# Two-block transformer kernel, one core: order of the first transfers, of the bias-row products and of the unread products at the head

## What is computed

```python
def rmsnorm(x, g):
    y = xf * lax.rsqrt(jnp.mean(xf * xf, axis=-1, keepdims=True) + EPS)
    return y * g
# layer 0 of the first block
h = h + even_mixer(rmsnorm(h, even_norm1[0]), even_w_in[0], ...)
qa, ka, va, qd, kd, vd = split_cols(h @ w_in, EVEN_IN_SPLIT)
bias = jnp.take(bias_table, rel_bucket(dist), axis=0)
```

## Times and profile before

| what | value |
|---|---|
| median of 3 runs | 3155.56 us (3153.17 to 3160.29) |
| profiled execution | 3161.49 us |
| its span, first to last instruction | 3159.6 us |
| PE busy | 96% of the span |
| DVE, ACT, POOL busy | 44%, 25%, 53% |
| mean granted TensorE clock | 0.983 |

### The profile page before, as it was taken

One profiled execution on the slowest core, in us unless ns is written; L12 is line 12 of the kernel. 1 busy time (PEld: TensorE's weight loads), 2 busy tenths in 40 slices (PEclk: granted clock), 3 DMA queues, 4 the chain that ended last, 5 costly groups with the idle time before them and its releaser, 6 DMA issues.

```text
span 3159.6 us, 44388 instructions
## 1 busy us (share of the span) xinstructions
PE 3033.1 (96%) x14692; PEld 2387.0 (76%) x14692; DVE 1399.9 (44%) x2391; ACT 792.1 (25%) x1451; POOL 1660.6 (53%) x1254
## 2 busy tenths in 40 slices
PE   8998999999899999989999999999889999999998
PEld 6767888886578888756678878888657688878886
DVE  3254444223444442452533476640744334576622
ACT  3342221113332210144421122210253411132201
POOL 4334666663156667423346656666323266646674
PEclk9998999999999999999999999999999999999999
DMA  6262223322022233211312222333112222223232
GB/s 161 77 173 67 93 94 106 110 90 74 21 73 93 97 102 110 70 34 53 102 61 99 83 75 95 99 104 103 48 41 75 67 90 100 83 73 100 94 115 77
DMA packets 99603, 274.90 MB, mean 87 GB/s; under 512 B 38126, under 2 KB 38894, under 8 KB 99490
## 3 DMA queue, kind: packets, MB, share of 16 engines
q1 hardware_dynamic: 97328, 269.07, 26.6%
q10 hardware_dynamic: 2162, 4.36, 0.8%
HBM read 269.66 MB, written 11.54 MB: 89 GB/s over the span
## 4 chain that ended last, share of the span: by engine, by line
PE 70%; DVE 3%; ACT 2%; issue 2%; DVEq 0%; ACTq 0%
PE PA L470 11%; PE PA L472 10%; PE PA L471 10%; PE PB L470 9%; PE PB L472 8%; PE PB L471 8%; PE O L736 2%; PE S L693 2%; PE T L604 2%; PE O L502 1%; DVE tmps L1398 0%; DVE hl L1359 0%; PE PB L753 0%; ACT probs L1128 0%; DVE strip L1782 0%
## 5 line engine op out<-in xcount | busy, mean ns | idle before, releaser
L452 POOL TENSOR_TENSOR wl<-raw,wh 128x1024 fp32r<-128x1024 f32 (+2 forms) x416 | 1128.0, 2711 | 33.4
L449 POOL TENSOR_TENSOR zero<-zero 128x1 f32<-128x1 f32 x416 | 82.7, 199 | 1434.3 <-PE PA L472 703.2
L470 PE MATMUL PA<-hh,wh 128*128 128x512 f32 x1392 | 567.1, 407 | 26.4 <-DVE hl L1359 7.1
L472 PE MATMUL PA<-hh,wl 128*128 128x512 f32 x1392 | 550.0, 395 | 0.0
L471 PE MATMUL PA<-hl,wh 128*128 128x512 f32 x1392 | 550.0, 395 | 0.0
L450 POOL CAST wh<-raw 128x1024 fp32r<-128x1024 f32 (+2 forms) x416 | 476.3, 1145 | 0.0
L470 PEld LDWEIGHTS PA<-hh,wh 128*128 128x128 f32 x1392 | 266.5, 191 | 135.5 <-issue 67.4
L470 PE MATMUL PB<-hh,wh 128*128 128x512 f32 x896 | 357.8, 399 | 0.0
L472 PE MATMUL PB<-hh,wl 128*128 128x512 f32 x896 | 349.4, 390 | 0.0
L471 PE MATMUL PB<-hl,wh 128*128 128x512 f32 x896 | 349.2, 390 | 0.0
L472 PEld LDWEIGHTS PA<-hh,wl 128*128 128x128 f32 x1392 | 265.8, 191 | 57.5
(11 more groups left out here) (314 smaller groups left out, 4750.2 us busy)
## 6 DMA issues: line engine op xcount, KB each, us to landing
raw<-in_w_up SPq DMA_DIRECT2D x176, 512.0 KB, 3.5
raw<-in_w_down SPq DMA_DIRECT2D x64, 768.0 KB, 4.1
raw<-in_w_merge SPq DMA_DIRECT2D x48, 768.0 KB, 4.1
raw<-in_w_out SPq DMA_DIRECT2D x32, 512.0 KB, 3.5
strips_na<-in_rpb SPq DMA_DIRECT2D x1, 7620.0 KB, 32.2
raw<-in_w_pool SPq DMA_DIRECT2D x12, 512.0 KB, 3.4
raw<-in_w_na_qk SPq DMA_DIRECT2D x12, 512.0 KB, 3.5
raw<-in_w_na_v SPq DMA_DIRECT2D x8, 512.0 KB, 3.6
```

The source lines that it names most:

```text
L449: nc.gpsimd.tensor_tensor(zero[:, :], zero[:, :], zero[:, :], ALU.add)
L452: nc.gpsimd.tensor_tensor(wl[s][:, 0:width], raw[s][:, 0:width], wh[s][:, 0:width].bitcast(F), ALU.subtract).then_inc(w_split, 1)
L470: mm(dst, h_, rh, start=first, stop=False)
L472: return mm(dst, l_, rh, start=False, stop=last)
```

## The change

The scale columns get a semaphore of their own (gains_in), their load comes directly after the first x transfer, and ACT and DVE wait for it instead of for all of const_in. The four other small loads go behind the four x transfers. SP issues the first pair of moba_v entries before the 8 tables. DVE clears acc as its very first instruction, makes the remainders hl before ubias and the dot products, and adds the squares after these. PE starts with four products of acc by acc into T0 that nobody reads, then makes the query half, then the two bias-row products, then the key half, and only after that waits for u_done. It issues four products more than before; everything else is the same work in another order.

```diff
-        NTABLE, NFIRST = 8, 5
+        NTABLE, NFIRST, FIRST_TURNS = 8, 4, 4
@@ SP
             entries("moba_q0", here("moba_q0"))
+            entry_pair("moba_v", here("moba_v"), 0, 0)
             for dst, src in tables:
                 sp.dma_start(dst, src).then_inc(table_in, 16)
-            entries("moba_v", here("moba_v"))
+            entries("moba_v", here("moba_v"), first=1)
@@ PE
+            pe.wait_ge(acc_done, 1)
+            for _ in range(FIRST_TURNS):
+                mm(T0[:, :], acc[:, 0:P], acc[:, :], start=True, stop=True)
+            qk_part(H("moba_q0"), 0, DT, H("moba_q0")["h"] - DT)
             pe.wait_ge(const_in, 16 * NFIRST)
             mm(S0[0:20, :], rel_sb, onehot[:, 0:S], start=True, stop=True).then_inc(u_ready, 1)
             mm(S1[0:20, 0:P], rel_sb, onehot[:, S:640], start=True, stop=True).then_inc(u_ready, 1)
+            qk_part(H("moba_q0"), DT, 2 * DT)
             pe.wait_ge(u_done, 1)
-            qk_part(H("moba_q0"), 0, 2 * DT, H("moba_q0")["h"] - DT)
@@ ACT
-            first = [(rel_sb, rel_in), (onehot, consts["onehot"]), (negmask, consts["negmask"]),
-                     (cols[:, :], cols_in), (lam[:, :], lam_in)]
+            first = [(rel_sb, rel_in), (onehot, consts["onehot"]), (negmask, consts["negmask"]), (lam[:, :], lam_in)]
             for j in range(0, DT, 2):
                 act.dma_start(x[:, j:j + 2, :], x_tiles[:, j:j + 2, :]).then_inc(x_arrived[j // 2], 16)
                 if j == 0:
-                    for dst, src in first:
-                        act.dma_start(dst, src).then_inc(const_in, 16)
+                    act.dma_start(cols[:, :], cols_in).then_inc(gains_in, 16)
+            for dst, src in first:
+                act.dma_start(dst, src).then_inc(const_in, 16)
-            act.wait_ge(const_in, 16 * NFIRST)
+            act.wait_ge(gains_in, 16)
@@ DVE
+            clear(here("x_in"))
             v.memset(eps[:, :], EPS).then_inc(dvc, 1)
+            dve.wait_ge(gains_in, 16)
+            b = here("x_in")
+            for j in range(DT):
+                remainder(b, j, CAT["even_norm1"])
             dve.wait_ge(const_in, 16 * NFIRST)
             dve.wait_ge(u_ready, 2)
...
-            b = here("x_in")
-            split_renewed(b, CAT["even_norm1"])
+            for j in range(DT):
+                add_squares(b, j, squares[:, j, :])
```

More of the change, by code:

```diff
@@ L283, in build @@
         den_ready, den_copied, diff_ready = sem("den_ready"), sem("den_copied"), sem("diff_ready")
-        const_in, table_in = sem("const_in"), sem("table_in")
+        const_in, gains_in, table_in = sem("const_in"), sem("gains_in"), sem("table_in")
         x_arrived = [sem(f"x_arrived{j}") for j in range(DT // 2)]
@@ L1002, in key_turn @@
                 mm(O1[:, :], perm[0][:, :], c3[3][:, :], start=True, stop=True).then_inc(kr_rot, 1)
+            H = here
+            ys = lambda k: (yh[:, k, :], yl[:, k, :])
+            pe.wait_ge(acc_done, 1)
+            for _ in range(FIRST_TURNS):
+                mm(T0[:, :], acc[:, 0:P], acc[:, :], start=True, stop=True)
+            qk_part(H("moba_q0"), 0, DT, H("moba_q0")["h"] - DT)
             pe.wait_ge(const_in, 16 * NFIRST)
@@ L1007, in _ @@
             mm(S1[0:20, 0:P], rel_sb, onehot[:, S:640], start=True, stop=True).then_inc(u_ready, 1)
+            qk_part(H("moba_q0"), DT, 2 * DT)
             pe.wait_ge(u_done, 1)
-            H = here
-            ys = lambda k: (yh[:, k, :], yl[:, k, :])
-            qk_part(H("moba_q0"), 0, 2 * DT, H("moba_q0")["h"] - DT)
             def moba_stat():
```

## The result

| | kernel before | changed kernel |
|---|---|---|
| median of 20 runs | 3153.66 us (3150.22 to 3160.29) | 3158.90 us (3151.26 to 3164.59) |
| ratio of the runs, 95% interval | 1 | 1.0017 (1.0011 to 1.0024) |
| span of the profiled execution | 3159.6 us | 3155.1 us |

The changed kernel is slower by 0.17%, 5.4 us (3.5 to 7.6, the interval times 3154). The one profiled execution of each points the other way: executions of one kernel lie up to 13 us apart, so a difference of this size is read from the median and from the place in the trace where work is late, never from two spans.

The account below looks back on a forecast made before the run. PE, busy 96% of the span, bounds the kernel, so its stream's start counts: value projection 1.3 us earlier, cut to 0.4 by the late strips and weights, 3155.56 - 0.4 = 3155.2 us; range 3150.0 to 3159.5.

Parts of the forecast that it names:

- a case that I held for less likely: Slower case: strips and next weights come later than forecast, a loss of 0.5 to 3 us, 3157.3; chance 0.18.
- Small loads: Head: ACT no longer waits for lam, so hh starts between 7 and 9.5 us, not 10.08; no gain credited.
- Remainders beside POOL: Head: DVE's remainders take turns with POOL's weight splits; the last comes at about 18.1 us, against 19.1 before.
- Unread products: PE's start: may raise the clock; query half ends at 18.8 us if kept, 20.2 to 21.0 if lost, 19.7 taken.
- Bias-row products and value projection: PE after the query half: products add 1.07 us; value projection starts at 26.2 against 27.50, 1.3 us earlier.
- Skew: ACT's transfer of ubias into the strips: issued at 22.2 us instead of 15.73, 6.5 later.
- Where the gain is taken back: Before the attention: the late skew shifts strips and next weights by 6.5 us, leaving a gain of 0.4, not 1.3.
- The strips' chain itself: SP's strips, then the next pair's weights: all shifted 6.5 us, weights issued at 43.8 and split by POOL at 51.1.
- Rivals: Strips' chain not late, gain 2 to 4.3 us, chance 0.27; chain later still, 0.18; clock not raised, 3156.4, 0.25 within forecast.
- the one on the slower side: Query half or const_in after 20.2 us makes PE wait at the first interleaved product: loss 0.5 to 3 us, chance 0.18.

Follow-up runs that it names:

- e3_staged: Changed kernel with the first skew done in two steps through DRAM, 32 copies outermost, to spread over 16 DMA engines; ratio 0.9986 to the kernel before.
- e7_hold_moved: Changed kernel, but ACT issues the skew only after the third value load has landed; ratio 1.0003 to the kernel before.
- e1_rows_first: Changed kernel with the bias rows back in front: small loads behind cols, bias-row products before the query half, ubias before remainders; ratio 0.9996 to the kernel before.
- e2_skew_late: Kernel before with one more wait on ACT, so the skew is issued only after two adds of squares; ratio 0.9999 to the kernel before.

## Why the prediction was wrong

I forecast a gain of 0.4 us; the measured loss is 5.4, inside my range of 3150.0 to 3159.5 but with the sign of a case that I held for less likely.

- *Small loads*: right. hh at 8.20, within 7 to 9.5.
- *Remainders beside POOL*: right in mechanism and size. Forecast last remainder at 18.1, measured 9.04 + 8.53 = 17.6.
- *Unread products*: right that it is open. The clock was neither kept nor lost for good: in the first execution it was 0.50 in 11 to 14 us and 1.00 from 15 on, in the other it was still 0.50 in 16 to 19. Query half at 18.6 in the first; in the other it ended 1.5 us later. I forecast 18.8 to 21.0.
- *Bias-row products and value projection*: right. Forecast 26.2, between 25.3 and 27.5; measured 25.41 and 26.89.
- *Skew*: right in time, 21.03 and 22.51 against 22.2.
- *Where the gain is taken back*: **the step that failed**. I followed the late skew only down its own queue: skew, strips, next weights. I took each weight load beside it at the 3.6 us of the earlier trace rows and wrote that the rest is "the same work in the same order". The value loads are issued beside the skew, and the kernel before already had the sign of it: the third one took 5.7 us from 26.86 and landed only at 32.6, behind the skew's last packets, although the skew left half of the engines' time free. The median of 5.4 us over the four value loads hid that. Nor did I ask how much slack that load had: 33.2 less 32.6, 0.6 us, and I pushed its end by 5.
- *The strips' chain itself*: a second fault in the same step, a wait read wrongly. I moved strips and weights by the whole 6.5 us of the skew, since I took the skew to end in 31 to 32 us, right before the strips' issue at 32.62. Its last packets were in 30 to 31 us. What SP was at until then was the fourth value load, which it could issue only when POOL's split of the second one was through, at 29.14 + 2.71 = 31.85. POOL and SP in the kernel before:

```profile
29.14 2.71 POOL L452 TENSOR_TENSOR wl<-raw,wh 128x1024 fp32r<-128x1024 f32 x1
26.86 5.50 SPq L339 DMA_DIRECT2D raw<-in_w_moba_v  x2
```

  So the skew had about 2 us of slack before it held the strips, not up to 0.6. e3_staged agrees: its skew landed near 29.7, and its strips went out at 32.26, behind POOL's split again. In the changed kernel the strips were 3.5 us later, not 6.5: SP's strips went out at 36.14 (forecast 38 to 39) and took 3.59 us, and the next weights at 41.15 waited for POOL's split, not for the strips. No idle time stands before the attention's first query product in the changed kernel. It would have been late in e7_hold_moved (next weights at 46.38, POOL waiting 2.24 us for them), and even there PE didn't wait.
- *Rivals*: the one on the slower side had the right cause upstream, a late skew, and a price of 0.5 to 3 us at another place. The case was worth 5.7 us: 3.94 of waiting and 1.7 of half clock behind it, less the 2.1 or 0.6 gained in the head, so 3.6 or 5.1 at the first score. That is within the interval of the 5.4 (3.5 to 7.6); what is left is not traced to a place. That the time fell into my range is luck: the range was wide for scatter and for another case, and none of its cases had this wait.

## What to carry to other kernels

A transfer that moves later is not only late itself: list every load that is issued while it runs, and look at what those loads took beside it before, one by one and not by their median. A load that lands only when a slow transfer ends, though engines are free, may be held by it; then its slack is the slack of the slow transfer. And before a chain is moved by what moves at its head, look which of two waits ended last: a step that waits for something else first (here the strips, behind POOL's split) moves by less. Where a slow transfer's outermost dimension is small, spreading it can be worth more than placing it (0.9986 for e3_staged against 0.9996 for e1_rows_first, with intervals that overlap).

## What the runs showed of the hardware that I had not expected

- Half of a 512 KB load moved in 3 us and the other half stood still for about 10, beside a transfer at 50 GB/s that used 47% of the DMA engines' time. The next load on the same queue got half of its bytes through in that time. Bandwidth was no limit (254 GB/s were moved in 37 to 38 us); the shared engines are the reading that fits all runs.
- The same 640 KB from 8 rows of SBUF took about 15 us, and from DRAM, with 32 outermost, 5.6 us; the load beside it took 3.5.
- A wait of PE can cost more than itself. After 3.94 us of waiting another 1.7 us went at half clock, after 2.54 us (e7_hold_moved) another 1.9, after 1.31 us (e2_skew_late) 0.2, with a granted clock of 1.00 throughout.
